# Latent attention: the keys of two heads in one product, and the swapped rotary columns among the query weights

## What is computed

```python
def mla_project(q_lat, kv_lat, g_qa, w_qb, g_kva, w_kvb):
    B, T = q_lat.shape[:2]
    q = (rms_norm_2(q_lat, g_qa) @ w_qb).reshape(B, T, H_B, NOPE_B + ROPE_B)
    kv = (rms_norm_2(kv_lat, g_kva) @ w_kvb).reshape(B, T, H_B, NOPE_B + V_B)
    return q[..., :NOPE_B], q[..., NOPE_B:], kv[..., :NOPE_B], kv[..., NOPE_B:]
...
    s = (jnp.einsum('bqhd,bkhd->bhqk', q_n, keys_n)
         + jnp.einsum('bqhd,bkd->bhqk', q_r, keys_r))
    p = jax.nn.softmax(s.astype(jnp.float32) * SCALE_B, axis=-1)
    return jnp.einsum('bhqk,bkhd->bqhd', p.astype(vals.dtype), vals)
```

## Time and profile before

| | us |
|---|---|
| median of 3 runs (3801.23 to 3804.77) | 3804.05 |
| the profiled execution, its own time | 3802.31 |
| its span, first to last instruction | 3800.3 |
| PE busy | 3578.9 (94%) |
| DVE busy | 2140.1 (56%) |
| ACT busy | 1413.3 (37%) |
| POOL busy | 742.6 (20%) |
| mean granted TensorE clock | 0.968 of full |

### The profile page before, as it was taken

How to read it: one execution, slowest core, us unless ns; L and a number is a source line. 1 busy time by engine, 2 the same in 40 slices (tenths; PEclk the granted TensorE clock), 3 DMA queues, 4 the chain that set the end, 5 groups by cost and what they waited for, 6 DMA issues and landing times.

```text
span 3800.3 us, 54861 instructions
## 1 busy us (share of the span) xinstructions
PE 3578.9 (94%) x21437; PEld 3045.6 (80%) x21437; DVE 2140.1 (56%) x4570; ACT 1413.3 (37%) x2301; POOL 742.6 (20%) x645
## 2 busy tenths in 40 slices
PE   7999998988999998999998999999999979999997
PEld 5877886878999998999996558867888845777886
DVE  3353443498989666887885354275333245537343
ACT  3232323323544443333334453164222345426222
POOL 0000000006987883555530000000000000000000
PEclk8999999999999998999998999999999989999998
DMA  6224333467888789999994001101212211120332
GB/s 221 95 78 144 95 99 122 141 211 253 296 283 285 279 300 345 368 362 346 359 360 152 23 29 56 62 18 41 65 62 67 89 56 40 62 83 23 100 95 94
DMA packets 220559, 594.55 MB, mean 156 GB/s; under 512 B 17936, under 2 KB 101520, under 8 KB 215952
## 3 DMA queue, kind: packets, MB, share of 16 engines
q1 hardware_dynamic: 156592, 380.68, 30.0%
q0 software_dynamic: 36864, 134.23, 9.8%
q10 hardware_dynamic: 26848, 76.14, 5.3%
HBM read 530.16 MB, written 60.82 MB: 156 GB/s over the span
## 4 chain that ended last, share of the span: by engine, by line
PE 79%; DVE 10%; DMA 6%; ACT 2%; issue 2%; POOL 1%; ACTq 0%; SPq 0%; DVEq 0%
PE bank L752 60%; PE bank L970 9%; DMA WR<-in_vrows 3%; PE bank L1064 2%; PE bank L1050 2%; PE bank L937 2%; DVE WL L1552 1%; PE bank L776 1%; PE bank L830 1%; DMA WR<-in_weights 1%; DVE hotA L1884 1%; DVE rows L1855 1%; DVE Rw L1824 1%; POOL rows L683 1%; DMA gelu_by_expert<-geU 1%
## 5 line engine op out<-in xcount | busy, mean ns | idle before, releaser
L1552 DVE TENSOR_TENSOR WL<-WR,WH 128x1024 fp32r<-128x1024 f32 x512 | 629.4, 1231 | 815.8 <-ACT WH L1158 758.9
L1158 ACT ACTIVATE WH<-WR 128x1024 fp32r<-128x1024 f32 x512 | 537.0, 1057 | 802.9 <-PE bank L970 204.8
L752 PE MATMUL bank<-H2h,WH 128*128 128x512 f32 (+2 forms) x1624 | 579.3, 357 | 4.5 <-DVE H2l L1580 4.5
L752 PE MATMUL bank<-H2h,WL 128*128 128x512 f32 (+2 forms) x1624 | 575.2, 354 | 0.0
L752 PE MATMUL bank<-H2l,WH 128*128 128x512 f32 (+2 forms) x1624 | 574.2, 354 | 0.0
L752 PE MATMUL bank<-Hh,WH 128*128 128x384 f32 (+1 forms) x1440 | 526.0, 365 | 26.3 <-DVE WL L1552 26.3
L752 PE MATMUL bank<-Hh,WL 128*128 128x384 f32 (+1 forms) x1440 | 511.0, 355 | 0.0
L752 PE MATMUL bank<-Hl,WH 128*128 128x384 f32 (+1 forms) x1440 | 510.2, 354 | 0.0
L970 PE MATMUL bank<-ah,WH 128*128 128x384 f32 x1024 | 344.9, 337 | 28.9 <-issue 17.9
L683 POOL DMA_INDIRECT rows<-in_urows,rk x128 | 171.3, 1339 | 965.5 <-DVE rk L1849 738.2
L752 PEld LDWEIGHTS bank<-H2h,WH 128*128 128x128 f32 (+1 forms) x1624 | 308.3, 190 | 50.6 <-issue 7.7
(11 more groups left out here) (318 smaller groups left out, 5600.3 us busy)
## 6 DMA issues: line engine op xcount, KB each, us to landing
WR<-in_weights SPq DMA_DIRECT2D x498, 512.0 KB
WR<-in_vrows SPq DMA_DIRECT2D x128, 512.0 KB
gelu_by_expert<-geU ACTq DMA_DIRECT2D x128, 192.0 KB
gates_by_expert<-tab ACTq DMA_DIRECT2D x24, 1024.0 KB
geV<-gelu_by_expert SPq DMA_DIRECT2D x32, 768.0 KB
Gt<-gates_by_expert SPq DMA_DIRECT2D x16, 1536.0 KB
x_kept<-X ACTq DMA_DIRECT2D x2, 3072.0 KB, 8.7
X<-x_kept ACTq DMA_DIRECT2D x2, 3072.0 KB, 11.2
```

Of the source, the lines that this page charges most:

```text
L752: yield nc.tensor.matmul(b[0:rows, out_cols], a, r, start=n == 0, stop=n == len(pairs) - 1)
L1158: act.activation(WH[:, n % SLOTS, :, :].rearrange("p a b -> p (a b)"), WR[:, c % SLOTS, :, :].rearrange("p a b -> p (a b)"), ACT.Copy)\
L1552: v.tensor_tensor(WL[:, n % SLOTS, :, :].rearrange("p a b -> p (a b)"), WR[:, plan.splits[n] % SLOTS, :, :].rearrange("p a b -> p (a b)"), ...
```

## The change

**Keys.** The weight chunk of an even head holds the key columns of that head and the next, 64 + 64. `hk` is done for even h alone, with 128 output rows. ScalarE copies rows 64 to 127 of the bank to rows 0 to 63 of the next head's key buffer, then rows 0 to 63 to this head's. There are four key buffers in place of two (`keys_of`: KH and KH2).

**Queries.** The query columns for x are 128 in place of 96: the last 32 are the rotary columns with their halves exchanged (the sign has moved into the table of sines). VectorE reads the bank itself (job hq x belongs to it now): cos times rows 0 to 95, sin times rows 96 to 127 on 32 rows, and an addition on 32 rows. R4's copy, the product with permB (hqp, krbp) and the constant permB with its load are gone; krb is treated in the same way.

```diff
@@ -82 +82 @@
-CONSTS = [("ident", 128), ("perm128", 128), ("permA", 128), ("permB", 96), ("iota128", 128), ("fold", 3)]
+CONSTS = [("ident", 128), ("perm128", 128), ("permA", 128), ("iota128", 128), ("fold", 3)]
@@ -310 +310 @@
-            p.job(("hq", l, h, "x"), "A")
+            p.job(("hq", l, h, "x"), "V", [] if upd or h % 2 == 0 else [("hb", l, h)])
@@ -312,4 +312,4 @@
-                p.job(("hq", l, h, "c"), "A")
-            p.job(("hk", l, h, "x"), "A")
-            p.job(("hk", l, h, "c"), "A", [("hb", l, h)])
-            p.job(("hqp", l, h), "V")
+                p.job(("hq", l, h, "c"), "A", [] if h % 2 == 0 else [("hb", l, h)])
+            if h % 2 == 0:
+                p.job(("hk", l, h, "x"), "A")
+                p.job(("hk", l, h, "c"), "A", [("hb", l, h)])
@@ -342 +342 @@
-            p.job(("krb", l, "x"), "A")
+            p.job(("krb", l, "x"), "V")
@@ -344 +343,0 @@
-            p.job(("krbp", l), "V")
@@ -511 +510 @@
-        qk_ready = sem("qk_ready")
+        qk_ready, kx_ready = sem("qk_ready"), sem("kx_ready")
@@ -580,0 +580 @@
+        KH2 = place("KH2", B0 + 19200, 2, A)
@@ -604,0 +605,4 @@
+        def keys_of(h):
+
+            return (KH, KH2)[h % 4 // 2][:, h % 2, :]
+
@@ -1005,2 +1009,2 @@
-                    wq = w[:, 0:QL * QKB].rearrange("p (k n) -> p k n", k=QL)
-                    wk = w[:, QL * QKB:QL * QKB + KVL * NOPE].rearrange("p (k n) -> p k n", k=KVL)
+                    wq = w[:, 0:QL * P].rearrange("p (k n) -> p k n", k=QL)
+                    wk = w[:, QL * P:(QL + KVL) * P].rearrange("p (k n) -> p k n", k=KVL)
@@ -1007,0 +1012 @@
+                        rows_ = P if c == "x" else QKB
@@ -1009,2 +1014,2 @@
-                                [(wq[:, j, :], LAT[:, j, xcols(c)]) for j in range(QL)], QKB)
-                    for c in ("x", "c"):
+                                [(wq[:, j, 0:rows_], LAT[:, j, xcols(c)]) for j in range(QL)], rows_)
+                    for c in ("x", "c") if h % 2 == 0 else ():
@@ -1012,4 +1017 @@
-                                [(wk[:, j, :], LAT[:, QL + j, xcols(c)]) for j in range(KVL)], NOPE)
-                    pe.wait_ge(act_read, k.reading(act_read, ("hq", l, h, "x")))
-                    product(("hqp", l, h), slice(0, T),
-                            [(consts["permB"][0:QKB, 0:QKB], R4[0:QKB, h % 3, :])], QKB)
+                                [(wk[:, j, :], LAT[:, QL + j, xcols(c)]) for j in range(KVL)])
@@ -1037 +1039 @@
-                                q, kk = col(QH[0:QKB, h % 2, :], qb), KH[0:QKB, h % 2, :]
+                                q, kk = col(QH[0:QKB, h % 2, :], qb), keys_of(h)[0:QKB, :]
@@ -1107,3 +1109 @@
-                    linear(("krb", l, c), ("krb", l), H2, xcols(c), QKB)
-                pe.wait_ge(act_read, k.reading(act_read, ("krb", l, "x")))
-                product(("krbp", l), slice(0, T), [(consts["permB"][0:QKB, 0:QKB], R4[0:QKB, 0, :])], QKB)
+                    linear(("krb", l, c), ("krb", l), H2, xcols(c), P if c == "x" else QKB)
@@ -1421,2 +1420,0 @@
-                    if h >= 3:
-                        act.wait_ge(dve_read, dve_at(("hqp", l, h - 3)))
@@ -1424,2 +1422 @@
-                        act.wait_ge(dve_read, dve_at(("krbp", l)))
-                    out_of(("hq", l, h, "x"), R4[0:QKB, h % 3, :], slice(0, T), rows=QKB)
+                        act.wait_ge(kx_ready, k.next(kx_ready))
@@ -1428,3 +1425,9 @@
-                    for c in ("x", "c"):
-                        out_of(("hk", l, h, c), KH[0:NOPE, h % 2, xcols(c)], slice(0, T if c == "x" else C), rows=NOPE)
-                    act.activation(KH[NOPE:QKB, h % 2, :], KR[NOPE:QKB, 0, :], ACT.Copy).then_inc(kr_ready, k.inc(kr_ready))
+                    for c in ("x", "c") if h % 2 == 0 else ():
+                        n_ = T if c == "x" else C
+                        act.wait_ge(filled, filled_at(("hk", l, h, c)))
+                        act.activation(keys_of(h + 1)[0:NOPE, xcols(c)],
+                                       bank[plan.by_key[("hk", l, h, c)].bank][NOPE:2 * NOPE, 0:n_], ACT.Copy)\
+                            .then_inc(act_step, k.inc(act_step))
+                        act.wait_ge(*k.own())
+                        out_of(("hk", l, h, c), keys_of(h)[0:NOPE, xcols(c)], slice(0, n_), rows=NOPE)
+                    act.activation(keys_of(h)[NOPE:QKB, :], KR[NOPE:QKB, 0, :], ACT.Copy).then_inc(kr_ready, k.inc(kr_ready))
@@ -1488 +1490,0 @@
-                out_of(("krb", l, "x"), R4[0:QKB, 0, :], slice(0, T), rows=QKB)
@@ -2008 +2010 @@
-                    dve.wait_ge(act_read, act_at(("hq", l, h, "x")))
+                    b = bank_of(("hq", l, h, "x"))
@@ -2014 +2016 @@
-                    v.tensor_tensor(QH[0:QKB, h % 2, 0:T], R4[0:QKB, h % 3, :], cosB[0:QKB, :], ALU.mult)\
+                    v.tensor_tensor(QH[0:QKB, h % 2, 0:T], b[0:QKB, :], cosB[0:QKB, :], ALU.mult)\
@@ -2016 +2018 @@
-                    v.tensor_tensor(t_[0:QKB, 0:T], bank_of(("hqp", l, h))[0:QKB, :], sinB[0:QKB, :], ALU.mult)\
+                    v.tensor_tensor(t_[NOPE:QKB, 0:T], b[QKB:P, :], sinB[QKB:P, :], ALU.mult)\
@@ -2020 +2022,2 @@
-                    v.tensor_tensor(QH[0:QKB, h % 2, 0:T], QH[0:QKB, h % 2, 0:T], t_[0:QKB, 0:T], ALU.add)\
+                    q_ = QH[NOPE:QKB, h % 2, 0:T]
+                    v.tensor_tensor(q_, q_, t_[NOPE:QKB, 0:T], ALU.add)\
@@ -2127,2 +2130,2 @@
-                dve.wait_ge(act_read, act_at(("krb", l, "c")))
-                v.tensor_tensor(KR[0:QKB, 0, 0:T], R4[0:QKB, 0, :], cosB[0:QKB, :], ALU.mult)\
+                b = bank_of(("krb", l, "x"))
+                v.tensor_tensor(KR[NOPE:QKB, 0, 0:T], b[NOPE:QKB, :], cosB[NOPE:QKB, :], ALU.mult)\
@@ -2130,5 +2133 @@
-                b = bank_of(("krbp", l))
-                v.tensor_tensor(QH[0:QKB, 0, 0:T], b[0:QKB, :], sinB[0:QKB, :], ALU.mult)\
-                    .then_inc(dve_step, k.inc(dve_step))
-                dve.wait_ge(*k.own())
-                v.tensor_tensor(KR[0:QKB, 0, 0:T], KR[0:QKB, 0, 0:T], QH[0:QKB, 0, 0:T], ALU.add)\
+                v.tensor_tensor(QH[NOPE:QKB, 0, 0:T], b[QKB:P, :], sinB[QKB:P, :], ALU.mult)\
@@ -2135,0 +2135,3 @@
+                dve.wait_ge(*k.own())
+                v.tensor_tensor(KR[NOPE:QKB, 0, 0:T], KR[NOPE:QKB, 0, 0:T], QH[NOPE:QKB, 0, 0:T], ALU.add)\
+                    .then_inc(kx_ready, k.inc(kx_ready))
@@ -2247,0 +2250 @@
+        out[:, :, QKB:P] = np.roll(out[:, :, NOPE:QKB], ROPE // 2, axis=2)
@@ -2255,3 +2258,5 @@
-        out[:, 0:QL * QKB] = tiles_of(a["w_qb_2"][l][:, h * QKB:(h + 1) * QKB])
-        w = a["w_kvb_2"][l][:, h * (NOPE + VB):h * (NOPE + VB) + NOPE]
-        out[:, QL * QKB:QL * QKB + KVL * NOPE] = tiles_of(w)
+        w = a["w_qb_2"][l][:, h * QKB:(h + 1) * QKB]
+        out[:, 0:QL * P] = tiles_of(np.concatenate([w, np.roll(w[:, NOPE:], ROPE // 2, axis=1)], axis=1))
+        if h % 2 == 0:
+            w = np.concatenate([a["w_kvb_2"][l][:, g * (NOPE + VB):g * (NOPE + VB) + NOPE] for g in (h, h + 1)], axis=1)
+            out[:, QL * P:(QL + KVL) * P] = tiles_of(w)
@@ -2280 +2285 @@
-    consts = np.concatenate([np.eye(P, dtype=f), swap(P, 64), swap(P, 32), swap(QKB, 16, NOPE),
+    consts = np.concatenate([np.eye(P, dtype=f), swap(P, 64), swap(P, 32),
@@ -2306 +2311 @@
-                           np.concatenate([zero, sb_, sb_, pad]), band], axis=1)
+                           np.concatenate([zero, pad, -sb_, sb_]), band], axis=1)
```

More of the change, by code:

```diff
@@ L2124, in branch @@
                     merge(b)
-                dve.wait_ge(act_read, act_at(("krb", l, "c")))
-                v.tensor_tensor(KR[0:QKB, 0, 0:T], R4[0:QKB, 0, :], cosB[0:QKB, :], ALU.mult)\
+                b = bank_of(("krb", l, "x"))
+                v.tensor_tensor(KR[NOPE:QKB, 0, 0:T], b[NOPE:QKB, :], cosB[NOPE:QKB, :], ALU.mult)\
                     .then_inc(dve_step, k.inc(dve_step))
-                b = bank_of(("krbp", l))
-                v.tensor_tensor(QH[0:QKB, 0, 0:T], b[0:QKB, :], sinB[0:QKB, :], ALU.mult)\
-                    .then_inc(dve_step, k.inc(dve_step))
+                v.tensor_tensor(QH[NOPE:QKB, 0, 0:T], b[QKB:P, :], sinB[QKB:P, :], ALU.mult)\
+                    .then_inc(dve_read, k.inc(dve_read))
                 dve.wait_ge(*k.own())
-                v.tensor_tensor(KR[0:QKB, 0, 0:T], KR[0:QKB, 0, 0:T], QH[0:QKB, 0, 0:T], ALU.add)\
-                    .then_inc(dve_read, k.inc(dve_read))
+                v.tensor_tensor(KR[NOPE:QKB, 0, 0:T], KR[NOPE:QKB, 0, 0:T], QH[NOPE:QKB, 0, 0:T], ALU.add)\
+                    .then_inc(kx_ready, k.inc(kx_ready))
                 inverted(("kvn", l), rk, A)
```

## The result

The changed kernel takes 3749.96 us (median of 4 runs, 3745.25 to 3752.06) against 3804.41 us before (4 runs); the ratio is 0.9853, 95% interval 0.9839 to 0.9866.

What follows compares the result with a forecast made beforehand. TensorE was taken to bound the latent attentions; 36.8 us removed, less 0.3 for loads and 0.9 for head 0, plus 0.3 at the start, gave 35.9 us less and 3768 us, range 3762 to 3779.

Steps and rivals of the forecast that it cites:

- What bounds the kernel at the change: Both latent attentions: TensorE sets the pace, so each us of its removed work is gained while other engines deliver in time.
- the sum: Whole kernel: 36.8 - 0.3 - 0.9 + 0.3 = 35.9 us gained, from removed work, loads, head 0 and start.
- The keys' term: Latent attention projections: key product done for 4 heads of 8 in each layer, 8 x 2.73 = 21.8 us less.
- The queries' term: Latent attention projections: permB's product gone from 8 heads in 2 layers, 16 x 0.94 = 15.0 us less.
- What is added to TensorE: Projections: weight loads grow to 128 columns, mostly hidden under the matmul before; 0.3 us in all.
- The upper bound of 5.9: Projections: 5.9 us added if none of the growth in weight loads were hidden.
- krbp: krb's product with permB, once a layer: its removal counted as nothing, at the most 1.9 us more for two.
- The even heads' chain: ScalarE and VectorE after even projections: no wait, 0.8 us spare in layer 0; rival of 3773 to 3777, chance 0.14 with dearer loads.
- the clock's: Latent attentions: rival that the granted clock falls to 1.2 GHz, making the kernel slower, for example 3839; chance 0.02.
- Head 0: First head of each layer: TensorE newly waits some 0.45 us for the exponential, 0.9 us together.
- Start: Kernel start: permB's load no longer holds ScalarE's queue ahead of XT's load; 0.3 us gained, of 0 to 0.6.
- More is gained: Whole kernel: rival of 3765 if krbp and all of permB's load count and head 0 doesn't wait; below 3763, chance 0.02.

## Why the prediction was right and wrong

- **What bounds the kernel at the change**: right. TensorE stayed busy for 99% of both latent attentions, and the removed work of both parts together was gained in full: 37.0 us where the sum had 35.6. The keys' term (21.8) measured 22.4 alone. The queries' term (15.0) came with the addresses in the time, 28.8 of 30. In the traces the two latent attentions are 343.9 us before, 322.8 with the keys alone, 332.2 with the queries alone and 306.9 with both. So the queries alone gave 11.7. Their projection got 0.91 us shorter a head (7.70 to 6.79 in layer 0), the units behind it 0.11 longer (14.13 to 14.24), and head 0 has new waits. On top of the keys they gave 15.9, and there the waits for R4's copy (3.0 us) go with them. Alone the two make 21.1 and 11.7, 32.8 us, and together 37.0.
- **What is added to TensorE**: taken as 0.3, it is nothing. The even projection is 0.2 us shorter than before, although its loads are wider. The upper bound of 5.9 would have needed unhidden loads, which this trace does not show. The same holds for the estimate of 6.0 by the Trainium skill (TensorE: Matmul & The Clock Gate, LDWEIGHTS): the 80 loads of 128 columns in layer 0's projections took 190 ns each, longer than its 107, and were hidden.
- **krbp**: right to count it as nothing. In the changed kernel TensorE waits 1.44 us ahead of the first squares' sums where the product with permB was.
- **The even heads' chain**: right, 2.2 and 4.4 us against 2.1 and 4.1, with no wait. This rival did not come, nor did the clock's: 0.99 over both windows, as before. The Trainium skill's remark (TensorE: Matmul & The Clock Gate, Part 4) that transposes do not engage the full clock gave that rival its condition. It did not come true here, in a stretch with transposes in every unit and other products between them; no run has a stretch of transposes alone, which would test the remark itself.
- **Head 0**: 1.4 us of waits for 0.9; the right place, and too small by 0.5.
- **Start**: 0.3 us was credited to permB's load. XT's load was issued 0.36 us sooner, but took 11.50 us where it had 10.89, so that this step gave nothing.
- **The step that failed is in the sum**: it counted permB's going as a product, a wait and 0.56 us of a queue, and put at nothing, without a reason, what its 384 bytes of SBUF do to the addresses of all tiles behind them. The experiments show 14 to 18 us for that, some 16 by the ratios over all chips. "More is gained" reached only to 3765, for other reasons. That the constant occupied 384 bytes ahead of the pool was in the diff. That Gt comes in pieces of 512 bytes was in the kernel, and that the DMA engines are at 96% during the expert sum was in the trace. With the addresses held, the forecast's 3768 was met by 3767, 3764 and 3769. The range was missed for this alone.

How the address acts is shown for Gt in part: a packet of 512 bytes takes 27.2 to 27.4 ns in the mean at a start of 0 or 256 and 29.1 to 30.3 at 64 or 384. 49152 of them at 2.7 ns more are 8.3 us of each of 16 engines, in a stretch that has these engines busy for 96%; Gt's address alone was worth 10 us. That the one makes the other is argued from these sizes. The Trainium skill, DMA: Bandwidth & Descriptors, section on how a descriptor splits into AXI transactions, says that a piece of data that does not start at a multiple of 256 bytes needs one transaction more; it tells this of reads, and here the written side was moved. The trace agrees with where the step lies. Its step is smaller, and it is not one that every packet takes: by the page's beats 64 would cost 12% and 384 25%, an estimate, while the means show 7% and 7 to 11%, and over half of the packets at 64 or 384 still take 27 ns. So why a start at 64 or 384 slows some packets and not others stays open. Which of the other tiles makes the remaining 6 us stays open. The medians of the 4096-byte packets were alike in all kernels, 159 ns. Only the 1280 packets of 2048 bytes follow the rest's address clearly, 87 ns against 84 in the median, which is 0.2 us of each DMA engine. No single other tile was moved.

## What to carry to other kernels

Removing or adding a small constant moves every tile that is allocated after it: look at the start addresses of DMA targets (for Gt's 512-byte pieces modulo 256) before reading a change's time as the work's, and keep the addresses fixed (a gap of the same size) when a part is to be measured. Where one engine is busy for 99% of a stretch and the chains of the others have spare time, its removed work comes back nearly in full: 37.0 us of 36.8 here for both parts together, though 11.7 of 15.0 for the queries alone. The chains at the even heads were summed in advance from their rows to within 0.3 us. A stretch with the DMA engines at 96% is worth a look in any change, even one that touches nothing in it.

## What was not expected of the hardware

384 unused bytes a partition cost 14 us of 3750. About 10 of the 16 us that all address runs give come with the tile written in packets of 512 bytes: 27.2 to 27.4 ns in the mean at a start that is a multiple of 256, 29.1 to 30.3 at 64 or 128 bytes beyond one, where a quarter to two fifths of them take over 30 ns and more than half still take 27. And reading partitions 96 to 127 or 64 to 127 while writing others cost neither VectorE (0.70 us) nor ScalarE (0.59 us) anything against the straight instruction.
